# Norm and choice stages by token tile, constant products on TensorE during the choices, and an eighth piece in the first experts' ring

## The reference, cut to what matters

```python
x = x + ga1 * _rmsnorm(mix, n_post_mix)                     # first block
h = _rmsnorm(x, n_pre_ffn) * (1 + sc2) + sh2                # scale and shift per feature
aff = softmax(h @ w_router)                                 # 512 x 16
gate, idx = top_k(aff.T, 64)                                # 64 tokens for each expert
hid = silu(xg @ w_gate[e]) * (xg @ w_up[e]);  yo = hid @ w_down[e]   # w: 1024x2048, 1024x2048, 2048x1024
...
h2 = rmsnorm(x, ffn_norm_g)                                 # second block: a scale alone
p_group = softmax(h2 @ w_group + b); fine = h2 @ w_router + b    # 4 groups, 32 experts
top-1 group, top-2 experts of its eight, weights; (silu(g) * u) @ w_down[e] for each token's two
```

## Time and profile before

| | us |
|---|---|
| median of 3 runs (lowest, highest) | 3634.04 (3626.78, 3643.66) |
| the profiled execution | 3636.84, its span 3634.9 |
| first norm and choice (from its first instruction to the first gather) | 1483.5 to 1547.1 |
| first experts | 1547.1 to 2517.8 |
| norm ahead of the second mixer | 2519.5 to 2546.6 |
| second norm and choice | 3288.6 to 3336.9 |
| second experts | 3338.4 to 3617 |
| mean granted TensorE clock | 0.929 |

### The profile page before, as it was taken

One profiled execution on the slowest core, in us unless ns is written; L12 is line 12 of the kernel. 1 busy time (PEld: TensorE's weight loads), 2 busy tenths in 40 slices (PEclk: granted clock), 3 DMA queues, 4 the chain that ended last, 5 costly groups with the idle time before them and its releaser, 6 DMA issues. The chain is left out here.

```text
span 3634.9 us, 38139 instructions
## 1 busy us (share of the span) xinstructions
PE 3149.1 (87%) x15784; PEld 1669.1 (46%) x15784; DVE 1072.0 (29%) x2063; ACT 558.7 (15%) x1166; POOL 283.7 (8%) x264
## 2 busy tenths in 40 slices
PE   6997889998998999698998999987996779996984
PEld 5444645664554444453344434433545763644331
DVE  2233702454573300310111011103146553422112
ACT  1002510112452200100000000001022221301111
POOL 0003000002751000000000000000002200001100
PEclk9999998998899999699999999998998989996997
DMA  7721021110001222369999999996310021016996
GB/s 262 255 70 47 2 73 35 46 36 0 24 1 47 93 70 69 163 293 427 411 420 414 422 424 412 425 423 262 127 35 2 3 101 55 12 58 247 409 424 268
DMA packets 132080, 669.33 MB, mean 184 GB/s; under 512 B 17578, under 2 KB 45645, under 8 KB 98889
## 3 DMA queue, kind: packets, MB, share of 16 engines
q1 hardware_dynamic: 115385, 630.24, 43.1%
q10 hardware_dynamic: 11488, 28.31, 2.1%
q0 software_dynamic: 5040, 8.40, 0.7%
HBM read 672.15 MB, written 14.69 MB: 189 GB/s over the span
## 5 line engine op out<-in xcount | busy, mean ns | idle before, releaser
L1961 PE MATMUL ec_wide<-ec_ring,ec_xg 128*64 128x512 f32 x2048 | 458.0, 601 | 24.9 <-issue 18.6
L1961 PEld LDWEIGHTS ec_wide<-ec_ring,ec_xg 128*64 128x64 f32 x2048 | 148.3, 138 | 314.6 <-issue 310.5
L1995 PE MATMUL ec_acc<-ec_ring,ec_hidT 128*64 128x512 f32 x1024 | 233.9, 611 | 40.5 <-DMA ec_ring<-in_w_exp_down 38.5
L2120 DVE TENSOR_SCALAR ec_xg<-ec_piece,ordered 128x128 f32<-128x128 f32 x64 | 21.9, 404 | 585.0 <-PE ec_piece L2009 585.0
L1995 PEld LDWEIGHTS ec_acc<-ec_ring,ec_hidT 128*64 128x64 f32 x1024 | 84.0, 141 | 188.4 <-issue 188.4
L3637 PE MATMUL hm_gu<-hm_ring,hm_xg 128*64 128x512 f32 x512 | 117.8, 614 | 12.1 <-DMA hm_ring<-in_moe_w_gu 9.5
L2009 PE MATMUL ec_piece<-ec_sel,x 128*128 128x128 f32 x512 | 124.4, 405 | 3.4 <-DVE ec_sel L2102 3.4
L2009 PEld LDWEIGHTS ec_piece<-ec_sel,x 128*128 128x128 f32 x512 | 122.9, 336 | 9.1 <-issue 5.7
L2685 POOL TENSOR_TENSOR solve_T<-const_rw,solve_T 128x512 f32<-128x512 f32 x8 | 10.1, 1265 | 1334.5 <-DVE solve_T L2723 1334.5
L2084 ACT ACTIVATE ec_hidT<-ec_acc 128x512 f32<-128x512 f32 x32 | 17.4, 594 | 523.1 <-PE ec_acc L1984 523.1
L1107 PE MATMUL conv_main<-hT,conv_early 128*128 128x512 f32 x192 | 86.8, 608 | 1.6 <-DVE bcT L1183 1.6
(11 more groups left out here) (616 smaller groups left out, 4975.6 us busy)
## 6 DMA issues: line engine op xcount, KB each, us to landing
ec_ring<-in_w_exp_gate SPq DMA_DIRECT2D x64, 2048.0 KB, 12.6
ec_ring<-in_w_exp_up SPq DMA_DIRECT2D x64, 2048.0 KB, 22.2
ec_ring<-in_w_exp_down SPq DMA_DIRECT2D x64, 2048.0 KB, 18.1
hm_ring<-in_moe_w_gu SPq DMA_DIRECT2D x32, 2048.0 KB, 25.3
hm_ring<-in_moe_w_down SPq DMA_DIRECT2D x16, 2048.0 KB, 28.5
ahead_qkv<-in_w_in SPq DMA_DIRECT2D x10, 2048.0 KB, 9.5
key<-in_w_ada ACTq DMA_DIRECT2D x4, 2048.0 KB
v<-in_w_ada ACTq DMA_DIRECT2D x4, 2048.0 KB, 10.3
```

What stands on the lines that cost most here:

```text
L1961: last = pe.matmul(wide[half(e), b, :], xg[:, u % 2, j, half(e)], w[e][:, a, b * 512:(b + 1) * 512], start=(j == 0), stop=(j == KD - 1))
L1995: last = pe.matmul(acc[half(e), h, :], hidT[:, f, half(e)], w[e][:, r, h * 512:(h + 1) * 512], start=(f == 0), stop=(f == FT - 1))
```

## The change

It does five things.

- **Token order.** RowNorm's turning goes by token tile t: TensorE waits for row tile t alone, makes eight transposes in two banks, VectorE takes the first bank and ScalarE the second, and `scores(t)` follows for that token tile (eight products). Takes stand between the rows on both engines (`dve_rows`, `act_rows`).
- **Scale in the weights.** In both choices the takes are plain copies. GpSimd multiplies the small router weights with the scale (`scaled`) and, in the first choice, sums weight times shift over the feature tiles (`shift`), which one more product for each token tile adds with a matrix of ones. In `mixer_rows` the scale stays in the takes: VectorE one 512-column product with a broadcast scale, ScalarE four 128-column activations.
- **Scratch.** `square` and `diag` lie in parts of xT that are written last, in `mixer_rows` in tiles of their own.
- **Constant products** (`keep_clocked`): products of ones with the identity, 128 columns, into a bank nobody reads: 12 after the first choice's scores, 72 after its turn, 48 after the second choice's scores, 12 ahead of `flips(0)`.
- **Ring.** EC_SLOTS 7 becomes 8.

```diff
+def keep_clocked(k, pe, bank, n):
+    for _ in range(n):
+        pe.matmul(bank[:, 0:P], k.const("ones"), k.const("ident"), start=True, stop=True)
...
+        def take(t):
+            act.wait_ge(self.tile_ready, 2 * t + 2)
+            if self.by_tokens:
+                act.activation(self.columns(t, 1), self.source(t, 1), ACT.Copy).then_inc(self.second_taken, 1)
+                return
+            for j in range(4):
+                ins = act.activation(self.columns(t, 1)[:, j, :], self.source(t, 1)[:, j, :], ACT.Copy, scale=self.scale[:, 4 + j:5 + j])
+            ins.then_inc(self.second_taken, 1)
...
             act.activation(self.rstd[:, t:t + 1], self.ss[:, t:t + 1], ACT.Sqrt, scale=1.0 / D, bias=eps).then_inc(self.root, 1)
+            if t:
+                take(t - 1)
+        take(LT - 1)
...
+            if t:
+                normed(t - 1)
+            if t >= 2:
+                take(t - 2)
+        normed(LT - 1)
+        take(LT - 2)
+        take(LT - 1)
...
-        pe.wait_ge(self.row_ready, LT)
-        for j in range(KD):
-            if j >= 4:
-                self.wait_tile(pe, j - 4)
-            for t in range(LT):
-                last = pe.transpose(self.pt[:, j % 4, t * P:(t + 1) * P], self.xn[:, t, j * P:(j + 1) * P], self.k.const("ident"))
+        for t in range(LT):
+            pe.wait_ge(self.row_ready, t + 1)
+            for h in range(2):
+                if t >= 2:
+                    pe.wait_ge(self.second_taken if h else self.first_taken, t - 1)
+                for j in range(4):
+                    last = pe.transpose(self.source(t, h)[:, j, :], self.xn[:, t, (4 * h + j) * P:(4 * h + j + 1) * P], self.k.const("ident"))
+                last.then_inc(self.tile_ready, 1)
+            if after is not None and t:
+                self.wait_tile(pe, t - 1)
+                after(t - 1)
...
-EC_SLOTS = 7
+EC_SLOTS = 8
...
+            pool.wait_ge(router_loaded, 16)
+            pool.tensor_tensor(shifted[:, :, :], w, sh.unsqueeze(2).to_broadcast([P, KD, E]), ALU.mult).then_inc(shifted_ready, 1)
+            pool.tensor_tensor(scaled[:, :, :], w, sc.unsqueeze(2).to_broadcast([P, KD, E]), ALU.mult).then_inc(scaled_ready, 1)
...
+            def scores(t):
+                if t == 0:
+                    pe.wait_ge(scaled_ready, 1)
+                    pe.wait_ge(shift_ready, 1)
+                for j in range(KD):
+                    pe.matmul(score[:, t * E:(t + 1) * E], norm.xT[:, t, j, :], scaled[:, j, :], start=(t == 0 and j == 0), stop=False)
+                last = pe.matmul(score[:, t * E:(t + 1) * E], k.const("ones"), shift[:, :], start=False, stop=(t == LT - 1))
...
             norm.turn(pe, scores)
+            keep_clocked(k, pe, norm.pt[:, 0, :], 12)
             pe.wait_ge(aff_ready, 1)
...
             last.then_inc(wide_ready, 1)
+            keep_clocked(k, pe, norm.pt[:, 0, :], 72)
             pe.wait_ge(chosen_T, 1)
...
             norm.turn(pe, scores)
+            keep_clocked(k, pe, norm.pt[:, 0, :], 48)
             pe.wait_ge(chosen_ready, 1)
...
             lists(1)
+            pe.wait_ge(index_ready, 2)
+            keep_clocked(k, pe, list_, 12)
             flips(0)
```

More of the change, by code:

```diff
@@ L2162, in _, with route_tokens @@
             dve.wait_ge(piece_taken, scatter_piece(u, SCATTERS - 1) + 1)
-def route_tokens(k, norm, out, router, ring, rank, aff):
+def route_tokens(k, norm, out, router, columns, ring, rank, aff):
     nc = k.nc
@@ L2198, in _ @@
         def _(pe):
[L2199 to L2205 removed]
+            def scores(t):
+                if t == 0:
+                    pe.wait_ge(scaled_ready, 1)
[3 more added lines that the diff above has]
+                last = pe.matmul(score[:, t * E:(t + 1) * E], k.const("ones"), shift[:, :], start=False, stop=(t == LT - 1))
+                if t == LT - 1:
                     last.then_inc(scored, 1)
             norm.turn(pe, scores)
+            keep_clocked(k, pe, norm.pt[:, 0, :], 12)
             pe.wait_ge(aff_ready, 1)
@@ L2233, in _ @@
         def _(dve):
-            norm.rows(dve)
-            norm.take_even(dve)
+            norm.dve_rows(dve)
             link = Steps(dve, step)
@@ L3410, in second_mixer, with route_experts @@
             low.close()
-def route_experts(k, norm, constants, ring, rank, place, first, share, rounds, xn_rows, ordered):
+def route_experts(k, norm, scale, constants, ring, rank, place, first, share, rounds, xn_rows, ordered):
     nc = k.nc
@@ L3450, in _, with scores @@
             sp.wait_ge(xn_stored, 16)
+        @block.gpsimd
+        def _(pool):
+            pool.wait_ge(loaded, 64)
+            pool.tensor_tensor(scaled[:, :, :], w[:, :, :], scale.unsqueeze(2).to_broadcast([P, KD, N]), ALU.mult).then_inc(scaled_ready, 1)
         @block.tensor
         def _(pe):
-            def scores(j):
-                if j == 0:
-                    pe.wait_ge(loaded, 64)
-                for t in range(LT):
-                    last = pe.matmul(score[:, t * N:(t + 1) * N], norm.xT[:, j, t * P:(t + 1) * P], w[:, j, :], start=(j == 0 and t == 0),
-                                     stop=(j == KD - 1 and t == LT - 1))
-                if j == KD - 1:
+            def scores(t):
+                if t == 0:
+                    pe.wait_ge(scaled_ready, 1)
+                for j in range(KD):
+                    last = pe.matmul(score[:, t * N:(t + 1) * N], norm.xT[:, t, j, :], scaled[:, j, :], start=(t == 0 and j == 0),
+                                     stop=(t == LT - 1 and j == KD - 1))
+                if t == LT - 1:
                     last.then_inc(scored, 1)
             norm.turn(pe, scores)
+            keep_clocked(k, pe, norm.pt[:, 0, :], 48)
             pe.wait_ge(chosen_ready, 1)
@@ L3806, in second_experts @@
                 constants = place_constants(k, s1, "moe")
-                h3T, xn = tile(s1, "hm_h3T", [P, KD, L]), tile(s1, "hm_xn", [P, LT, D])
-                route_experts(k, RowNorm(k, out, h3T, scale, xn=xn), constants, ring, rank, place, first, share, rounds, xn_rows, ordered)
+                h3T, xn = tile(s1, "hm_h3T", [P, LT, KD, P]), tile(s1, "hm_xn", [P, LT, D])
+                route_experts(k, RowNorm(k, out, h3T, xn=xn), scale, constants, ring, rank, place, first, share, rounds, xn_rows, ordered)
             dump("hm_rank", rank)
```

135 lines of the change are left out of this document (63 added, 72 removed).

## The result

The kernel after takes 3610.64 us (median of 6 runs, 3606.14 to 3614.04), the kernel before 3633.92 (6 runs). The ratio is 0.9932, 95% interval 0.9919 to 0.9945: 23.3 us faster, where 28.6 were forecast. The profiled execution took 3611.27 us, with a span of 3609.3.

The account below looks back on a forecast made before the run. First experts bound by their weights, both choices by uncovered chains. Gains 2.6 + 19.3 + 2.4 + 4.3 = 28.6 us take the profiled 3636.84 to 3608.2; that execution stood 2.8 above the median, so 3605.4 us, range 3584 to 3622.

Parts of the forecast that it names:

- The term of 19.3 us: First experts' weight stream: eighth slot saves 4.9 us for its piece and 14.4 in five stretches at 368 to 405 GB/s.
- the piece's own time: Eighth piece lands in the first choice's idle time, so one less stands behind the first freed piece: minus 4.9 us.
- the lead: Eighth slot gives the queue 4.9 us more lead, covering five slow stretches lacking 1.6 to 4.2 each: minus 14.4 us.
- Part 1: First choice by token tile: turns and scores run without a wait inside, scores end 4.9 us earlier.
- The constants, first choice: 12 products hold the turn, plus 3.3; 72 hold the turn back, plus 1.9; counting minus 2.3, turns minus 0.6 us.
- Part 3: Mixer norm, turn and takes alone: minus 2.4 us, bounds minus 3.5 and plus 1.
- Part 4: Second choice to hidden(0): scores -3.9, 48 constants +3.7, counting -3.2, 12 constants +1.7, higher clock -2.6; sum minus 4.3 us.
- Slots were not what was missing: Rival: first experts' slow stretches come from queue or memory, the slot gives only 4.9 us: 3619.8 us, chance 0.14.
- no overlap: Rival: each scores(t) waits for takes behind VectorE's row work, norms keep their length: plus 11.2, 3616.6 us, chance 0.06.
- constants at half clock: Rival: clock does not rise on the constants, first choice 16 us longer, second 10: 3638 us, chance 0.06.
- The clock rises in the scores: Rival: full clock midway in both choices' scores, first 5 and 2.3, second 4.5 and 2.4 us: 3591.2 us, chance 0.2.
- The port pair: First choice: GpSimd's sums may block VectorE by a shared port lock, under 2 us together, hidden by TensorE's backlog.

Follow-up runs that it names:

- experiment 1: Kernel before with EC_SLOTS 8 instead of 7 and nothing else of the change: 3617.89 us, 0.9968 of before.
- experiment 2: Kernel after with EC_SLOTS 7 instead of 8, so norms, choices and constants alone: 3630.65 us, 0.9996 of before.
- experiment 5: Kernel after with the eighth piece not loaded during the choice but only once gate(0, 0) has freed pieces: 3616.38 us, 0.9961 of before.
- experiment 6: Kernel after with EC_SLOTS 6 instead of 8: 3658.47 us, 1.0073 of before.
- experiment 9: Kernel after, second ring first loaded with seven pieces, the last two after GpSimd's first-step reloads, no 12 constants ahead of flips(0): 3610.74 us, 0.9938 of before.
- experiment 10: As experiment 9, with the choices' constant products cut from 12 to 3, 72 to 60 and 48 to 30: 3595.06 us, 0.9907 of before.
- experiment 3: Kernel after with all four groups of constant products out: 3613.82 us, 0.9949 of before.
- experiment 4: Kernel after with constant products cut from 12 to 3, 72 to 52 and 48 to 30: 3607.94 us, 0.9946 of before.
- experiment 8: Kernel after, second ring first loaded with seven pieces, the last two issued when the first gather has landed: 3608.86 us, 0.9936 of before.

## Why the prediction was right, and where it was not

**The bound was read rightly.** The first experts are bound by their weights, and the five slow stretches lacked slots. The term of 19.3 us measured 19.2 against the trace it was made from, and 13.7 against a second one. Experiments 1, 2, 5 and 6 part it: the piece's own time 3.9 (forecast 4.9), the lead 10 to 15 (14.4). The time read from one trace of a stream that runs short is uncertain by 6 us, which the forecast did not say.

**Part 1** measured 5.1 for 4.9: turns at 0.21 us, nine products and no wait inside.

**The constants, first choice.** Price and place were right: 4.73 us for the 12 (forecast 4.9), 16.24 for the 72 (15.5), counting 2.40 (2.2), in sum 2.4 to the end of the counting (2.6). The two holds were 2.8 us (3.3) and 2.6 us (1.9). The mis-sized term stands behind it, where I had put nothing: `gate(0, 0)` took 8.8 us, not 7.1. In before it ran at full clock throughout; after, part of it is at half:

```profile
1536.00:1539.00 3.00, 0.00 (x0) 0.00 (x0) 1.73 (x8) 1.28 (x1) 0.00 (x0) 0.50 0.00 0
1557.00:1560.00 3.00, 3.00 (x10) 0.85 (x8) 1.19 (x6) 0.00 (x0) 0.00 (x0) 0.58 0.00 0
```

Between the gather and `gate(0, 0)` TensorE waits 1.46 us for `ec_xg` in both kernels. In before the clock stayed full over this wait, in after it fell. So 2.4 us at the counting are 0.7 at the first freed piece. That the constants brought this about is not shown: in experiment 1 the clock fell at the same place without them. What the forecast lacked is a bound for it.

**Part 3** measured 3.0 for 2.4. The term that was off is ScalarE's takes, four in 1.14 us against my 0.46 us each:

```profile
2515.06 1.14 ACT L320 ACTIVATE h2mT<-mixer_rows_pt,vec_second 128x128 f32<-128x128 f32 x4 [1.54 <-PE mixer_rows_pt L393]
```

**Part 4 failed.** It forecast minus 4.3 and measured plus 1.9. Up to the issue of the gather the sum was right: scores 4.0 earlier (3.9), constants 13.77 us (12.7), counting 3.2 (3.0), gather 2.6 earlier (3.4). The step that failed is the sentence that gather and reloads "come under a busier queue" and "beside the constants this is covered". The gather took 7.8 us to land instead of 4.6 in before. No gather of the kernel after landed sooner than 6.3 us behind its issue (all sixteen, L3639):

```profile
DMA to landing us min/median/max: 6.3/10.4/11.6
```

The nine pieces and the store of the normed rows keep the queue full to some 59 us behind the stage's start. In the seven traces with the new order and nine pieces, the two reloads of the first step were issued at 44 to 56 us and landed at 58 to 60. Experiment 2 shows it at its clearest (10.8 us earlier in, 1.3 earlier out), 9 and 10 take the cause away. What would have shown it ahead is a comparison that I did not make: in the trace of before the gather was issued at 3342.4 and landed at 3347.0, and the stretch from 3343 on flows at 68 GB/s: the first load ends just as the gather comes. A chain that ends beside the end of a transfer may not be the one that holds.

The second mis-sized term is the clock that the 12 constants ahead of `flips(0)` were to carry into `hidden(0)`, 2.6 us. The flips took 1.17 us, but the clock was at half again behind them, with waits of 1.35 and 1.32 us on both sides, and `hidden(0)` took 10.02 us where it was 8.8 before. Without any constants (experiment 3) it took 9.87, so the 12 carried nothing into it. This makes 1.0 us of the 1.9 that the stage is longer; the rest lies behind `hidden(0)`, where two profiles of the kernel after differ by as much.

**The rivals.** *Slots were not what was missing* and *no overlap* did not occur, nor did *constants at half clock*. *The clock rises in the scores* did, in the second choice and in three of the ten traces with the new order of the norms (experiments 2, 6 and 10), never in the first choice. The turns and scores from 8 us behind the stage's start on, 76 and 78 instructions, in windows of experiment 2:

```profile
3281.90:3290.00 8.10, 8.10 (x76) 8.10 (x76) 3.54 (x6) 4.04 (x7) 0.00 (x0) 1.00 0.99 421
```

and of the kernel after:

```profile
3268.20:3284.30 16.10, 16.10 (x78) 16.10 (x78) 3.65 (x6) 4.06 (x7) 0.00 (x0) 0.50 0.99 404
```

It gave up to 10.8 us at the gather, not the 4.5 plus 2.4 of the rival, and next to nothing at the end until the queue was cleared (the stage took 347.2 us in experiment 2).

**The number.** 3605.4 against 3610.6: part 4 is off by 6 us, the way from the counting to the first freed piece by 2, and the slot's term by nothing or by 6, after which of the two traces of before it is measured. The faster stretch ahead of the first choice, 2 to 8 us of the 23.3, covers some of that and is no part of the mechanism: that the time came so near is in part luck.

**The port pair.** The forecast weighed that GpSimd's sums might block VectorE. In the kernel after they lie beside its steps:

```profile
1481.13 0.25 POOL L2229 TENSOR_TENSOR route_shifted<-route_shifted 128x32 f32<-128x32 f32 x1
1481.18 1.28 DVE L367 SCALAR_TENSOR_TENSOR branch<-branch,route_brstd,route_spread 128x1024 f32<-128x1024 f32 x1 [0.45 <-PE route_spread L384]
...
1483.95 1.28 DVE L367 SCALAR_TENSOR_TENSOR branch<-branch,route_brstd,route_spread 128x1024 f32<-128x1024 f32 x1
```

VectorE's step took 1.28 us with them and 1.28 without. It has an operand in PSUM, though, so the lock that the Trainium skill (SBUF — State Buffer, "SBUF: two separate sides") describes for two SBUF inputs is not put to the test here.

## What to carry to other kernels

A ring of slots is to be judged at its worst stretch, not by its mean: sum up what each slow stretch lacks, and give slots until that is gone. Work that shortens a chain is worth nothing while small transfers of the same chain are queued among a bulk load; either the bulk load leaves room for them, or it waits for them. Work that only keeps TensorE busy pays for a short consumer right behind it and must end neither before nor after the step that it bridges: 52 products left 1.48 us free and lost the clock in the counting, 72 held the chain by 2.6 us, 60 by 0.3 and kept the clock. Even so the 1.7 us that 60 gained on 52 at the counting were gone one step later, when `gate(0, 0)` lost its clock: such a gain counts only where it reaches the next thing that is waited for.

## What the runs showed of the hardware

- **A short pause and the clock.** TensorE stood still for 1.48 us behind 12 us of constants at granted clock 1.00, and 20 small products right behind ran at half, 4.42 us. A pause of 1.46 us ahead of `gate(0, 0)` left the clock full in before and in experiment 4, and half in after and in experiment 1. The length of the pause alone does not tell. The Trainium skill (TensorE: Matmul & The Clock Gate, "What's actually happening"), by which activity releases the throttle, agrees as to the direction, but it does not tell these cases apart.
- **The same work at either clock.** From 8 us on, turns and 36-column scores of the second choice ran wholly at 0.50 or wholly at 1.00, both with TensorE busy all the time. In the traces where it rose (2, 6 and 10) the clock had fallen earlier, 0.5 us behind the stage's start; in the seven of the same order where it stayed at half it had fallen at 2.5 to 2.6 us. That is a coincidence in ten traces; no run tested it. In the first choice TensorE was busy for 20.3 us without a pause, with turns and 16-column scores, and stayed at 0.50 in all ten: there being busy did not release the clock.
- **GpSimd's indirect transfers** are slow by what is queued beside them. A reload landed 2.2 us behind its issue in experiment 9, when the queue was all but empty, and 14 to 15 us behind it in experiments 2 and 6, among whole pieces. The first gather took 4.4 and 4.5 us in experiments 9 and 8, and 7.8 to 10.4 in the kernel after and the others with nine pieces.
